# The sample tile of a token-major unit: eight fp32 products of the raw weights on four column groups, ahead of its unit's prompt tiles

## The reference, cut to what matters

```python
D_MODEL, SEQ, DEC_SEQ, DEPTH = 1024, 512, 32, 2
def mixer_inputs(h, pos, p):
    q_r, k_r, v_r, g_r, q_d, k_d, v_d, ga, gb = jnp.split(h @ p['w_in'], points, axis=-1)
    q_r = rope(q_r.reshape(B, L, N_RET_HEADS, RET_DK), pos, RET_DK, RET_ROPE_THETA)
    k_r = rope(k_r...) * (RET_DK ** -0.5)
    q_d = rope(rmsnorm(q_d, p['q_norm_g']), pos, DIFF_ROT, ROPE_THETA)
    k_d = rope(rmsnorm(k_d, p['k_norm_g']), pos, DIFF_ROT, ROPE_THETA)
    return (q_r, k_r, v_r, g_r), (q_d, k_d, v_d), (ga, gb)
def layer_prompt(x, pos, p, lam_init):      # h = rmsnorm(x, norm1_g) for 512 rows
def layer_sample(x, pos, ck, cv, ...):      # the same weights for 32 rows
```

## Time and profile before

| | |
|---|---|
| Time, median of 3 runs (lowest to highest) | 2290.76 us (2290.44 to 2292.8) |
| The profiled execution's own time | 2291.64 us |
| its span in the profile | 2289.8 us |
| TensorE's mean granted clock | 0.998 |
| Busy: PE, PEld | 2255.5, 2145.7 us |
| Busy: DVE, ACT, POOL | 1145.5, 968.5, 856.9 us |
| Read from and written to memory | 177.50, 13.42 MB |

### The profile page before, as it was taken

How to read it: one execution, slowest core, us unless ns; L and a number is a source line. 1 busy time by engine, 2 the same in 40 slices (tenths; PEclk the granted TensorE clock), 3 DMA queues, 4 the chain that set the end, 5 groups by cost and what they waited for, 6 DMA issues and landing times.

```text
span 2289.8 us, 42591 instructions
## 1 busy us (share of the span) xinstructions
PE 2255.5 (99%) x17512; PEld 2145.7 (94%) x17512; DVE 1145.5 (50%) x1903; ACT 968.5 (42%) x1829; POOL 856.9 (37%) x378
## 2 busy tenths in 40 slices
PE   6999999999999999999999999999999999999998
PEld 6889889999999999999998899899999999999998
DVE  5665563444545554156255665633354556623553
ACT  4554553434323443254245544533343234423443
POOL 3343232333334343443452343223244343343433
PEclk9999999999999999999999999999999999999999
DMA  4232222222222222322322231322212222223222
GB/s 162 66 108 75 89 66 93 72 69 73 75 77 90 93 87 65 105 88 76 101 88 90 67 108 56 106 67 72 81 61 74 93 80 87 82 78 111 84 73 97
DMA packets 81648, 193.66 MB, mean 85 GB/s; under 512 B 7504, under 2 KB 36528, under 8 KB 81456
## 3 DMA queue, kind: packets, MB, share of 16 engines
q1 hardware_dynamic: 59696, 173.50, 23.2%
q10 hardware_dynamic: 21760, 17.45, 2.3%
HBM read 177.50 MB, written 13.42 MB: 83 GB/s over the span
## 4 chain that ended last, share of the span: by engine, by line
PE 94%; POOL 2%; DVE 2%; ACT 1%; issue 1%; DMA 0%; ACTq 0%; DVEq 0%
PE ps L600 14%; PE ps L602 13%; PE ps L601 13%; PE ps L639 6%; PE ps L640 6%; PE ps L641 6%; PE ps L999 4%; PE ps L998 4%; PE ps L1000 4%; PE ps L666 2%; PE ps L781 2%; PE ps L739 2%; PE ps L816 2%; PE ps L747 2%; PE ps L872 2%; PE ps L740 1%
## 5 line engine op out<-in xcount | busy, mean ns | idle before, releaser
L483 POOL TENSOR_TENSOR wlo<-raw,whi 128x1024 fp32r<-128x1024 f32 (+1 forms) x330 | 769.0, 2353 | 1206.8 <-ACT whi L1056 1206.8
L600 PE MATMUL ps<-hl,whi 128*128 128x272 f32 x2432 | 703.7, 289 | 0.0
L602 PE MATMUL ps<-hl,wlo 128*128 128x272 f32 x2432 | 700.6, 288 | 0.0
L601 PE MATMUL ps<-hl,whi 128*128 128x272 f32 x2432 | 699.1, 287 | 0.0
L600 PEld LDWEIGHTS ps<-hl,whi 128*128 128x128 f32 x2432 | 458.9, 189 | 1.5
L602 PEld LDWEIGHTS ps<-hl,wlo 128*128 128x128 f32 x2432 | 457.4, 188 | 0.0
L601 PEld LDWEIGHTS ps<-hl,whi 128*128 128x128 f32 x2432 | 456.9, 188 | 0.0
L1056 ACT ACTIVATE whi<-raw 128x1024 fp32r<-128x1024 f32 (+1 forms) x330 | 313.4, 997 | 212.0 <-PE ps L1000 177.7
L639 PE MATMUL ps<-whi,hl 128*128 128x256 f32 x1216 | 349.9, 288 | 2.9 <-POOL wlo L483 2.0
L640 PE MATMUL ps<-wlo,hl 128*128 128x256 f32 x1216 | 343.1, 282 | 0.0
L641 PE MATMUL ps<-whi,hl 128*128 128x256 f32 x1216 | 342.7, 282 | 0.0
(11 more groups left out here) (228 smaller groups left out, 3436.7 us busy)
## 6 DMA issues: line engine op xcount, KB each, us to landing
raw<-in_w_units_dram SPq DMA_DIRECT2D x260, 512.0 KB, 4.7
raw<-in_w_down_units_dram SPq DMA_DIRECT2D x64, 352.0 KB, 3.4
out_new_k_prompt_dram<-rawk ACTq DMA_DIRECT2D x8, 512.0 KB, 6.3
out_new_v_prompt_dram<-vd ACTq DMA_DIRECT2D x8, 512.0 KB, 5.5
raw<-in_w_first_dram SPq DMA_DIRECT2D x6, 512.0 KB, 4.7
out_y_dram<-x SPq DMA_DIRECT2D x8, 272.0 KB, 6.1
kc_n<-in_cache_k_dram SPq DMA_DIRECT2D x8, 256.0 KB, 2.9
vc_n<-in_cache_v_dram SPq DMA_DIRECT2D x8, 256.0 KB, 3.5
```

The source lines that it names most:

```text
L483: e.tensor_tensor(wlo[:, s, a:b], raw[:, s, a:b], whi[:, s, a:b].bitcast(F32), ALU.subtract).then_inc(*S.up("w_ready", ("lo", j, part)))
L600: e.matmul(out, wh, hi, start=(c == 0), stop=False)
L601: e.matmul(out, wh, lo, start=False, stop=False)
L602: ins = e.matmul(out, wl, hi, start=False, stop=(c == KC - 1))
```

## The change

The sample tile is computed in another way and at another place. `xs` becomes the sum of both halves, 32 fp32 columns per chunk, made by DVE. The tile is eight fp32 products with `raw`, chunk c into the rows 32 (c % 4) of the bank, so it has four row blocks of partial sums. ACT's rest copy takes block 1 as before, DVE adds blocks 2, 3 and 0 in three instructions instead of one. The tile needs neither `whi` nor `wlo`, waits for the load alone, and comes first in its unit; the unit's end is noted at prompt tile 3. In the fill it is one entry after the gate tiles, ahead of q's. Loads of `raw` now also wait for the sample tile of the unit that lies in the slot. Some banks and the places of the sums in DVE's queue change with it.

```diff
-        xs = sb("xs", [P, KC, 2, DEC], F32R)
+        xs = sb("xs", [P, KC, DEC])
-        D_BANKS = dict(k=("mm0", "mm1", "t", "mm0", "o"), v=("mm1", "mm0", "mm1", "mm0", "o"))
+        D_BANKS = dict(k=("mm0", "mm1", "o", "mm0", "t"), v=("mm1", "mm0", "mm1", "mm0", "o"))
+        TILE_ORDER = (NT,) + tuple(range(NT))
...
                 e.wait_ge(*S.at("w_ready", k=2 * j - 4))
+                if phase == "D" and j == 1:
+                    e.wait_ge(*S.at("mm_ready", k=-NT if S.index else 0))
+                if phase == "D" and j > 1:
+                    e.wait_ge(*S.at("mm_ready", ("N", j - 2, NT)))
...
+            def sample_products(bank, s):
+                for c in range(KC):
+                    rows = slice(DEC * (c % 4), DEC * (c % 4 + 1))
+                    ins = e.matmul(ps[rows, BANK[bank]:BANK[bank] + UC], xs[:, c, :], raw[:, s, c * UC:(c + 1) * UC],
+                                   start=(c < 4), stop=(c >= 4))
+                return ins
...
-                for m in range(TILES):
+                for m in TILE_ORDER:
...
-        FILL = ([("g", t, c) for t in range(4) for c in range(KC)] + [("q", t, c) for t in range(NT) for c in range(KC)]
-                + [("s", 0, c) for c in range(KC)])
+        FILL = ([("g", t, c) for t in range(4) for c in range(KC)] + [("s", 0, KC - 1)]
+                + [("q", t, c) for t in range(NT) for c in range(KC)])
-        FILL_SHARE = (5, 5, 5, 4, 4, 5, 5, 5, 4, 4)
+        FILL_SHARE = (5, 5, 4, 4, 4, 5, 5, 4, 4, 1)
...
-                e.activation(xs[:, :, :, :].rearrange("p c v s -> p (c v) s"),
-                             hl1[:, :, :, SEQ:TOK].rearrange("p c v s -> p (c v) s"), ACT.Copy).then_inc(*S.up("xs_ready", "xs"))
...
                 def sample_sum(buf, bank, key, *name):
                     e.wait_ge(*S.at(f"act_free_{bank}", ("rest",) + key))
+                    for g in (2, 3):
+                        e.wait_ge(*S.own())
+                        e.scalar_tensor_tensor(out=rest[:, :], in0=ps[g * DEC:(g + 1) * DEC, BANK[bank]:BANK[bank] + UC],
+                                               scalar=rs1[0:DEC, NT:TILES], in1=rest[:, :], op0=ALU.mult, op1=ALU.add).then_inc(
+                                                   *S.up("dve_step"))
...
                 for _ in S.bodies("S"):
+                    e.wait_ge(*S.own())
+                    e.tensor_tensor(xs[:, :, :], hl1[:, :, 0, SEQ:TOK].bitcast(F32), hl1[:, :, 1, SEQ:TOK].bitcast(F32), ALU.add).then_inc(
+                        *S.up("dve_step", key="xs"))
...
-                    qk_apply(rawq, "q", 0, lambda: sample_sum(rawk[0:DEC, NT, :], "o", ("N", 0, 4), "k"))
+                    sample_sum(rawk[0:DEC, NT, :], "t", ("N", 0, 4), "k")
+                    qk_apply(rawq, "q", 0)
                     qk_sums("k")
+                    sample_sum(vd[0:DEC, NT, :], "o", ("N", 1, 4), "v")
                     qk_apply(rawk, "k", 1)
-                    sample_sum(vd[0:DEC, NT, :], "o", ("N", 1, 4), "v")
...
                         if n + 2 < 10:
                             maxes(n + 2)
                         weights_of_sample(n)
-                    e.wait_ge(*S.at("s_ready", ("q", 1)))
-                    sample_sum(rawq[0:DEC, NT, :], "mm1", ("N", 3, 4), "q'")
+                        if ("s", 0) in filled_at(n):
+                            e.wait_ge(*S.at("s_ready", ("q", 1)))
+                            sample_sum(rawq[0:DEC, NT, :], "mm1", ("N", 3, 4), "q'")
...
+                        if hh + 1 < RET_HEADS:
+                            sample_sum(rk[0:DEC, NT, :], f"mm{(t0 + 14) % 2}", ("N", 3 * hh + 2, 4), hh + 1, 0)
```

More of the change, by code:

```diff
@@ L641, in n_tile, with n_unit @@
                         ins = e.matmul(out, lo, wh, start=False, stop=(c == KC - 1))
-                    ready(ins, ("N", j, m))
+                    ready(ins, ("N", j, m), *([("end", j)] if m == NT - 1 else []))
                 else:
[L644 to L651, removed]
-                for m in range(TILES):
+                    raw_here(j)
+                    ready(sample_products(bank, slot(S.phase, j)), ("N", j, m))
+            def n_unit(j, X, dve=False, before=None, after=None, chunk=None, banks=(None,) * TILES):
+                for m in TILE_ORDER:
                     if before:
@@ L655, in n_unit @@
                     if m == NT:
-                        n_tile(j, m, X, XS, act=1, dve=1, bank=banks[m])
+                        n_tile(j, m, X, act=1, dve=1, bank=banks[m])
                     else:
-                        n_tile(j, m, X, XS, act=int(not dve), dve=int(dve), chunk=chunk if m in (0, 2) else None, bank=banks[m])
+                        n_tile(j, m, X, act=int(not dve), dve=int(dve), chunk=chunk if m in (0, 2) else None, bank=banks[m])
                     if after:
@@ L691, in pe_program @@
                     stats("t")
[L692 to L698, removed]
+                    e.wait_ge(*S.at("dve_step", "xs"))
+                    ready(sample_products(S_BANKS[NT], 0), ("N", 0, NT), ("end", 0))
                 for p in S.bodies("D"):
@@ L727, in fill @@
                             u = 2 if kind == "g" else 3
[L728 removed]
+                            if kind == "s":
+                                raw_here(u)
+                            elif t == 0:
                                 weights(u, c)
[L730 removed]
+                            if c == 0 or kind == "s":
                                 filled[1] = mm_bank()
@@ L749, in fill @@
                                 ins = e.matmul(out, lo, wh, start=False, stop=(c == KC - 1))
-                                keys = [("N", 3, t)]
+                                keys = [("N", 3, t)] + ([("end", 3)] if t == NT - 1 else [])
                             else:
[L752 to L756, removed]
+                                ins = sample_products(bank, s)
+                                keys = [("N", 3, NT)]
                             if c == KC - 1:
@@ L1846, in gated @@
                                                 *S.up(f"dve_free_{bank}", key))
+                        bank = f"mm{(t0 + 9) % 2}"
+                        e.wait_ge(*S.at(f"act_free_{bank}", ("rest", "N", 3 * hh + 1, 4)))
+                        for g in (2, 3):
+                            e.wait_ge(*S.own())
+                            e.tensor_tensor(rest[:, :], ps[g * DEC:(g + 1) * DEC, BANK[bank]:BANK[bank] + UC], rest[:, :], ALU.add).then_inc(
+                                *S.up("dve_step"))
+                        e.wait_ge(*S.own())
+                        e.tensor_tensor(rest[:, 0:UC], pv(bank, DEC, UC), rest[:, 0:UC], ALU.add).then_inc(
+                            *S.up(f"dve_free_{bank}", ("gsum", hh)))
                         gate(0)
```

94 lines of the change are left out of this document (46 added, 48 removed).

## The result

The changed kernel takes 2305.69 us (median of 4 runs, 2305.19 to 2306.78) against 2290.71 us (4 runs, 2290.44 to 2292.8): a ratio of 1.0064, 95% interval 1.0051 to 1.0077. It is slower by 15 us, where 7 us less were forecast. The profiled execution took 2305.29 us.

A forecast was written before the change was run, and what follows sets the result against it. TensorE's queue was taken as the bound. R -17.2, six bodies +5.4, two bodies +2.7 and clock +1.5 gave -7.6 us from 2291.64: 2284. The forecast's own range was 2274 to 2296, the whole range 2262 to 2320.

The forecast's parts named there:

- its own signs: Prediction wrong if the tile body is over 1.1 us or if TensorE's two forecast waits in D are missing.
- What bounds the kernel: Whole kernel: TensorE, busy 99% of the span with 94% of the last chain, so time off its queue counts.
- The new tile: Sample tile on TensorE: four column groups overlap, passes take 0.86 us, tile 0.98 or 1.18 instead of 1.82.
- the double switch: Sample tile paying for both stationary-shape changes: 1.18 us, against 0.98 where its neighbour forces one anyway.
- B: Every sample tile: passes start in program order, only neighbours overlap, 1.94 us instead of 0.86; about 2320; chance 0.16.
- C: Every sample tile: column groups don't overlap, 3.44 us per tile; 2382; chance 0.08.
- R: Phase R's 22 sample tiles, all on the path, no new wait: -17.2 us.
- k and v: D, bodies 1 to 3: TensorE waits 1.3 us at the fifth gate chunk; of 1.5 us only 0.15 kept.
- The start of the layers: Body 0: S, k, v savings become waiting, +0.3 per layer; layer 0's late D start costs nothing; layer 1 clock +1.5.
- The q' tile: D, fill 2: three sums delay combine 3, transpose 3 moves +2.16, later fill -1.1; +1.05 us per body.
- The loads: Loads of raw now wait for the sample tile but stay hidden; if not, a few us per unit.
- Rival A: Waits in D don't bind: 2255 without both, 2271 to 2276 without one; chance 0.20.

The follow-up runs named there:

- pairs: q_sum_later with each sample tile's eight products ordered 0 0 1 1 2 2 3 3 over the column groups; one profile, 2271.75 us.
- later_xs: q_sum_later with DVE adding up xs ahead of the lambda arithmetic, for layer 1 at the end of G; 2271.93 us.
- pool_held: Changed kernel plus a wait on POOL: lo of D's fourth prepared unit starts only when DVE's combine 3 is done; 2308.48 us.
- q_sum_later: Changed kernel with DVE's three q' sums one step later, behind combine 3 and the maxes of step 5; 2272.59 us.
- early_held: early_lo plus a wait on POOL: lo of the gate unit starts only when DVE's rope q is done; 2265.58 us.
- early_lo: q_sum_later with the gate unit's hi ahead of v's second prompt tile and its lo ahead of the power of k; 2281.16 us.

## Why the prediction was wrong

2284 was forecast, 2305.69 measured: slower by 15 us where 7 less were forecast. By its own signs the prediction would have stood: the tile is under 1.1 us, and both waits are in D, 1.14 us at the gate tile in bodies 1 to 3 and 2.85 us at step 3 in all 8. The step that failed is the price of the second wait. It was put at 1.7 us, with no clock loss behind it.

**What bounds the kernel**: right. TensorE's queue, and D's own chains a few tenths behind it.

**The new tile**: right. 1.00 to 1.01 us wherever it stands in D and R, against 0.98 and 1.18. Where the neighbours on both sides are prompt tiles (133.47 to 134.47 in body 1) it takes 1.00 too, so the double switch was 0.18 too dear. The four groups overlap. Rivals B and C are out: `pairs` shows that a group's second product doesn't hold back the next group, which was B's mechanism. The estimate by the 2.38 times for three column tiles in the Trainium skill, "TensorE: Matmul & The Clock Gate", Part 3, was 1.09 for the passes alone; that is above the whole measured tile.

**R**: right, -17.2 forecast, -17.1 between the traces, 16.9 by itself; no wait. The close match is partly luck: with 1.00 per tile the same working gives -18.0, and 0.18 per head (2.28 measured, 3 x 0.82 = 2.46) is not located. Rope of head 2 ends at 472.65 and its transposes start at 475.19: 2.54 us of room, 2.5 forecast.

**k and v**: right. The wait at the fifth gate chunk was put at 1.3 and is 1.14, the stretch grew by 1.43, and about nothing is kept.

**The start of the layers**: body 0 was to lose 0.3 more than the others; by the starts on TensorE's timeline it is 1.0 in layer 0, and 1.8 in layer 1 with its clock loss, for which 1.5 + 0.3 stood. The first prompt tile of D starts at 39.20, where 35.6 stood, and nearly all of that is taken up before the end of body 0. What takes it up no run separates: `later_xs` moves the wait to bank t, which the prediction doesn't mention. Here too a stall lies ahead: the two lambda steps, 2.54 us long in the earlier trace rows, last 4.29 us beside lo, and xs and the reading of bank t stand behind them.

**The q' tile**: this is the step that failed: combine 3 "now ends at 170.4", a wait of 1.7 us, "Per body +1.05". The place, the order and the queue behind it were right, and so was the end of the three sums (18.6 us behind the k transposes in both). But combine 3 was moved as a block of 1.2 us, as long as it had been, without asking what runs beside it at its new place: L1750 took 1.35 instead of 0.22, +1.13 in 8 bodies, 9 us. And a clock loss of 1.5 us was added in one place of layer 1, behind a wait of 3 us, and none behind the 8 waits of this kind; six of them had one, 1.5 us each, 9 us more. Together 18 of the 21 us between -7.6 and +13.7. The rest is small: the segment behind step 3 and the start of layer 0.

The Trainium skill has the rule for the first, in "SBUF — State Buffer", section "Who interferes with whom": a DVE instruction with two SBUF inputs contends with a GpSimd instruction that reads SBUF, and the port pair they share is an exclusive lock. The traces agree: L1750 (two inputs, sums and rinv) and rope's L1695 stall; the sums L1651 and L1655 (one input in PSUM) and the reciprocal L1748 (one) run at 0.50, 0.47 and 0.17 beside the same lo. Over the whole trace of the changed kernel it is the same: L1907 (128 x 5, two inputs in SBUF) takes 0.17 alone and 2.34 to 2.36 beside lo, L2034 (128 x 272, one input in PSUM) 0.44 in both places. L1764 in `pool_held` (2.57 instead of 0.49) has one input, and for it the same section of the Trainium skill names another reason: a tensor_scalar from SBUF to SBUF can run in a mode that takes both ports. The rule bears on this change, and the prediction didn't draw on it. The profile before had the same in its own rows: apply's steps of 1280 columns took 1.49 us for q, alone, and 3.67 and 3.57 for k, beside lo; and a step of one column took 1.65 (L1745, above).

**The loads**: right. No load stands in TensorE's list of waits.

**Rival A** was wrong for this kernel: both waits bind. Its price for a kernel without one of them, 2271 to 2276, fits q_sum_later (2272.6), which of the two has only the gate wait.

**The chances**: 0.20 for A and two thirds of 0.56 add up to 0.57 for a faster kernel, not 0.54.

Open: why the clock stays up in body 2 of both layers behind a wait of 2.85 us. Not tried: the rest copy of q' ahead of hi, and another bank for k's sample tile in body 0.

## What to carry to other kernels

When an instruction moves, look up what POOL does at its new time, not only how long the instruction took at the old: a step of 0.2 us can last until its long neighbour ends. Price a new wait on TensorE at its length plus a low-clock stretch behind it, here 1.5 us behind waits of 2.85 us in 6 of 8 places. When a wait is removed, look in the list of waits whether it has gone or moved to the next place. A partial sum that nobody needs soon goes behind the step that TensorE needs next; and a wait added on a third engine, so that it starts its long instruction after a row of short ones, can gain more than an earlier start (early_held against early_lo: 15.6 us).

## What the runs showed of the hardware

Four column groups of 32 stationary columns take fp32 passes at the same time, 0.215 us each, 16 in 1.0 us with both switches; the order in the program doesn't matter (1.01 and 1.02), only how many passes the fullest group gets (10: 2.28). Beside a piece of POOL's lo (2.35 us), which reads two SBUF tensors, a DVE step with two inputs in SBUF ends about when the piece does (within 0.25 us): one column of 0.22 us lasted 1.35, 160 columns of 0.33 lasted 2.55. A step with one input in PSUM kept its time (0.47, 0.50). Behind waits of 2.85 us TensorE's granted clock went to its lower level in 6 of 8 bodies (0.84 and 0.59 in two windows of 3 us), at a cost of 1.5 us each; behind the waits of 1.14 us it stayed at 1.00.
